# First norm of a layer: TensorE multiplies x by a diagonal of the row factors, in place of scaled copies and transposes

## Chip, cores and metric

One core of one Trainium2 chip. The metric is device time of one execution in microseconds.

## What is computed

A trunk of two layers on 256 tokens of width 1024. Only the first step of each layer is touched by the change:

```python
def rmsnorm(x, g):
    xf = x.astype(jnp.float32)
    y = xf * lax.rsqrt(jnp.mean(xf * xf, axis=-1, keepdims=True) + EPS)
    return (y * g.astype(jnp.float32)).astype(x.dtype)
...
    for l in range(DEPTH):
        h = rmsnorm(x, norm1_g[l])
        x = x + mixing_block(h, ...)      # first product: h @ w_in[l]
        h = rmsnorm(x, norm2_g[l])
        x = x + hier_moe(h, ...)
```

Everything is float32. The matrix products after the norm need h with channels on the partitions, while x is held with tokens on the partitions, so the norm ends in a turn of x by 90 degrees.

## The kernel before

**Tiling.** The tokens are two tiles of 128 (`T = 2`), the channels eight groups of 128 (`KT = 8`). Channel group k is not a run of neighbours: it takes channels k, k + 8, k + 16 and so on, so that a group read straight from x has a step of eight floats (32 bytes) in a partition.

**Split products.** Weights come from memory as float32 "units" of 128 x 2048. ScalarE makes the high part `w_hi` (helper `hi`, line 522), VectorE the low part `w_lo` (helper `lo`, line 839). h is split the same way into `h_hi` and `h_lo` (which live in the tiles `a_hi` and `a_lo`), and each product is three matmuls (lines 1380 to 1382). Each engine's program is written out by hand in its own order, with semaphores between them. No planner is involved: an instruction waits, and all that stands behind it on the same engine waits too.

**The first norm of a layer, step by step.**

1. ScalarE squares x and sums each row (line 545 in layer 0, line 532 in layer 1), after the row tile has been loaded or, in layer 1, after VectorE has added the last sums to x (line 1363).
2. VectorE adds the halves and the epsilon (line 864), GpSimd raises to the power -0.5 (line 464 in layer 0, once per token tile; line 507 in layer 1, both at once). The factor of each row is in `rs1`.
3. The scaled copy `xn` of x is written group by group, x being read with the step of eight: VectorE (line 869) does all of token tile 0 and groups 4 to 7 of tile 1; ScalarE (`scale_part`, line 537) does groups 0 to 3 of tile 1.
4. TensorE transposes the 16 blocks of `xn` (line 1407) into banks 4 to 7 of PSUM: bank 4 + k % 4 holds groups k and k + 4. After the last transposes into a bank the semaphore `n1_t` goes up by one.
5. ScalarE reads the turned groups, multiplies by the gains and writes `h_hi` (line 556). VectorE writes `h_lo` (line 905).
6. TensorE starts the products with `w_in`. In layer 0 the first two units go through `first_products` (lines 1445 to 1456), which first waits for `w_hi` of the unit as a whole and then, for each k, for `h_lo` of that group; eight matmuls with the high weights per k, and those with `w_lo` at the end. In layer 1 it is the ordinary loop (lines 1380 to 1382), twelve matmuls per k.

**Order around it.** While TensorE waits for steps 1 to 3 it multiplies a matrix of ones (`keep_warm`, line 1393): 14 matmuls before the transposes of layer 0, 16 before those of layer 1, and 6 more in layer 0 after the transposes. In layer 0 ScalarE runs `scale_part`, then `hi` of unit 0, then step 5; VectorE does `h_lo` of groups 0 to 3, then `lo` of unit 0, then `h_lo` of groups 4 to 7. In layer 1 the high parts of units 0 and 1 and the low part of unit 0 were made ahead, in the expert part of layer 0. SyncE issues all weight transfers; those of units 0 to 3 come before the norm of layer 0, and the change does not move any.

Of the kernel before, what the change touches and what calls it, by code (L numbers as in the profile page):

```python
# [25 lines left out]
ALU = mybir.AluOpType  # L26
ACT = mybir.ActivationFunctionType
AX = mybir.AxisListType.X

P = 128  # L30
# [10 lines left out]
def trunk(nc, x_in, positions, norm1_g, w_in, sgu_ln_g, sgu_ln_b, sgu_w, sgu_b, q_norm_g, k_norm_g, sinks,  # L41
# [4 lines left out]
    T = SEQ // P  # L46
    KT = D // P
# [65 lines left out]
    with ExitStack() as ctx:  # L113
# [14 lines left out]
        x = sb("x", [P, T, D])  # L128
        a_hi = sb("a_hi", [P, 2048], F32R)
        a_lo = sb("a_lo", [P, 2048], F32R)  # L130
        xn = sb("xn", [P, T, KT, P])
# [33 lines left out]
        ident = sb("ident", [P, P])  # L165
# [19 lines left out]
        rs1 = sb("rs1", [P, T])  # L185
# [43 lines left out]
        diag = flat_g[:, 7168:7168 + SEQ].rearrange("p (t s) -> p t s", t=T)  # L229
# [31 lines left out]
        bank = [ctx.enter_context(nc.psum_tensor(f"bank{i}", [P, 512], F32)) for i in range(8)]  # L261
# [9 lines left out]
        pool_consts = sem("pool_consts")  # L271
# [5 lines left out]
        def S(name):  # L277
            if name not in names:
                names[name] = sem(name)
            return names[name]  # L280
# [233 lines left out]
        def _(act):  # L514
            a = nc.scalar

            def hi(at, n):
                slot = at.raw(n)
                act.wait_ge(landed[slot], at.landed(n))
                act.wait_ge(unit_used, at.ring(n))  # L520
                w = width(n, at.moe)
                a.activation(w_hi[:, at.part(n), 0:w], raw_at(slot)[:, 0:w], ACT.Copy).then_inc(hi_done, 1)  # L522
# [9 lines left out]
                a.activation(sq_dump[:, t, 512 * h:512 * h + 512], x[:, t, 512 * h:512 * h + 512], ACT.Square,  # L532
                             scale=float(D ** -0.5), accum_out=ssqh[:, t, h:h + 1]).then_inc(S("n1_ssq"), 1)

            def scale_part(l):
                act.wait_ge(S("n1_rs"), T * (l + 1))
                a.activation(xn[:, 1, 0:4, :], x[:, 1, :].rearrange("q (p c) -> q c p", c=KT)[:, 0:4, :], ACT.Identity,
                             scale=rs1[:, 1:2]).then_inc(S("n1_xa"), 1)

            act.wait_ge(pool_consts, 1)  # L540
            a.activation(warm[:, 0:1], ones[0:1, 0:1], ACT.Square)
            act.wait_ge(S("ssq_zero"), 1)
            for t in range(T):
                act.wait_ge(x_loaded[t], 16)
                a.activation(sq_dump[:, t, :], x[:, t, :], ACT.Square, scale=float(D ** -0.5),
                             accum_out=ssqh[:, t, 0:1]).then_inc(S("n1_ssq"), 2)
            scale_part(0)
            hi(At(0, 0, False), 0)
            act.wait_ge(S("tab_zero"), 1)
            for l in range(DEPTH):  # L550
                act.wait_ge(par_g, 16 * (l + 1))
                for k in range(KT):
                    act.wait_ge(S("n1_t"), 4 * l + k % 4 + 1)
                    if k >= 4:
                        act.wait_ge(S("h_lo_done"), KT * l + k - 3)
                    a.activation(h_hi[:, k, :], bank[4 + k % 4][:, 256 * (k // 4):256 * (k // 4) + 256], ACT.Identity,
                                 scale=g1[:, k:k + 1]).then_inc(S("h_hi_done"), 1)
                before = act.value_load(tab[0:1, 0, 7:8], min_val=0, max_val=DEPTH * (NG + 1)) if l else 0
                at = At(l, before, False)
                if l == 0:  # L560
# [10 lines left out]
                for t in range(T):  # L571
                    last = a.activation(v_n[:, t, :], bank[1][:, MIX * t:MIX * t + MIX], ACT.Gelu_apprx_tanh,
                                        accum_out=v_mu[:, t:t + 1])
# [80 lines left out]
                for c in range(CT):  # L654
                    a.activation(d_sig[:, c, :], d_acc[:, c, :], ACT.Silu, bias=cols[:, c, K31 + 2:K31 + 3],
                                 scale=cols[:, c, K31 + 1:K31 + 2]).then_inc(S("yd_done"), 1)
# [164 lines left out]
                if l < DEPTH - 1:  # L821
                    for i in range(2 * T):
                        act.wait_ge(S("x_out"), 2 * T * l + i + 1)
                        square(i % 2, i // 2)
                    scale_part(l + 1)

# [2 lines left out]
        def _(dve):  # L831
            v = nc.vector
# [28 lines left out]
            def rstd_rows(l):  # L861
                for t in range(T):
                    dve.wait_ge(S("n1_ssq"), 2 * T * l + (t + 3 if l else 2 * t + 2))
                    v.tensor_scalar(ms1[:, t:t + 1], ssqh[:, t, 0:1], ssqh[:, t, 1:2], EPS, ALU.add,
                                    ALU.add).then_inc(S("n1_ms"), 1)
                for t in range(T):
                    dve.wait_ge(S("n1_rs"), T * l + t + 1)
                    k = 4 * t
                    v.tensor_scalar(xn[:, t, k:, :], x[:, t, :].rearrange("q (p c) -> q c p", c=KT)[:, k:, :],
                                    rs1[:, t:t + 1], None, ALU.mult).then_inc(S("n1_x"), 1)  # L870

            rstd_rows(0)

            def rope_angles():
# [27 lines left out]
            for l in range(DEPTH):  # L902
                for k in range(KT):
                    dve.wait_ge(S("h_hi_done"), KT * l + k + 1)
                    v.scalar_tensor_tensor(out=h_lo[:, k, :], in0=bank[4 + k % 4][:, 256 * (k // 4):256 * (k // 4) + 256],  # L905
                                           scalar=g1[:, k:k + 1], in1=h_hi[:, k, :].bitcast(F32),
                                           op0=ALU.mult, op1=ALU.subtract).then_inc(S("h_lo_done"), 1)
                    if l == 0 and k == 3:
                        lo(At(0, 0, False), 0)

                before = dve.value_load(tab[0:1, 0, 7:8], min_val=0, max_val=DEPTH * (NG + 1)) if l else 0
# [83 lines left out]
                for k in range(K3):  # L995
                    for c in range(CT):
                        w = cols[:, c, K31 + 3 + k:K31 + 4 + k]
                        src = bx[:, c, k:k + SEQ]
                        if k == 0:
                            last = v.tensor_scalar(yc[:, c, :], src, w, None, ALU.mult)  # L1000
                        else:
                            last = v.scalar_tensor_tensor(out=yc[:, c, :], in0=src, scalar=w, in1=yc[:, c, :],
                                                          op0=ALU.mult, op1=ALU.add)
# [352 lines left out]
                for i in range(2 * T):  # L1356
                    t, h = i % 2, i // 2
# [13 lines left out]
        def _(pe):  # L1371
            mm = nc.tensor.matmul
            tp = nc.tensor.transpose
# [17 lines left out]
            def keep_warm(b, n):  # L1391
                for _ in range(n):
                    mm(bank[b][:, 0:P], ones[:, :], ones[:, :], start=True, stop=True)
# [3 lines left out]
            pe.wait_ge(S("zero_done"), 1)  # L1397
            pe.wait_ge(S("tab_zero"), 1)
            for l in range(DEPTH):
                keep_warm(4, 16 if l else 14)  # L1400
                for t in range(T):
                    pe.wait_ge(S("n1_x"), T * l + t + 1)
                    if t:
                        pe.wait_ge(S("n1_xa"), l + 1)
                    for k in (0, 4, 1, 5, 2, 6, 3, 7):
                        c = 256 * (k // 4) + P * t
                        last = tp(bank[4 + k % 4][:, c:c + P], xn[:, t, k, :], ident[:, :])
                        if t == T - 1 and k >= 4:
                            last.then_inc(S("n1_t"), 1)
                if l == 0:  # L1410
                    keep_warm(3, 6)

# [47 lines left out]
                for b in range(4):  # L1460
                    for h in range(2):
# [10 lines left out]
                        for kk in range(4):  # L1472
                            k = 4 * h + kk
                            fi, la = k == 0, k == KT - 1
                            if b == 0:
# [3 lines left out]
                                for t in range(T):  # L1479
                                    last = tokens(1, both(wp, kk, slice(256, 512)), k, t, fi and t == 0, la,  # L1480
                                                  256 * t, 256, True)
                            elif b == 1:
                                for t in range(T):
                                    last = tokens(2 + t, both(wp, kk), k, t, fi, la)
                            else:
                                for f in range(4):
                                    last = channels(2 * (b % 2) + f // 2, wp, k, kk, f, fi, la)
                        last.then_inc(unit_used, 1)
                pe.wait_ge(S("win_act"), 7 * l + 5)
                for h in range(2):  # L1490
                    ready(at, 8 + h)
                    wp = [w[:, 0:4, :] for w in parts(at, 8 + h, "p (c m) -> p c m", c=8)]
                    for kk in range(4):
                        for f in range(2):
                            last = channels(0, wp, 4 * h + kk, kk, f, h == 0 and kk == 0, 4 * h + kk == KT - 1)
# [47 lines left out]
                for h in range(NQ):  # L1543
                    last = score(bank[4][:, P * h:P * h + P], h, 0, 0)
# [4 lines left out]
                for i in range(2):  # L1549
                    for h in (2 * i, 2 * i + 1):  # L1550
                        for tk in range(T):
                            c = 256 * (h % 2) + P * tk
# [139 lines left out]
                for k in range(2):  # L1692
                    last = project_half(1, k)
# [185 lines left out]
```

## Time and profile before

| | us |
|---|---|
| median of 3 runs | 784.68 |
| lowest, highest of the runs | 784.68, 784.87 |
| the profiled execution, its own time | 784.63 |
| its span, first to last instruction | 782.9 |
| granted TensorE clock over the span | 0.999 |
| TensorE busy (matmul) | 772.4 |
| VectorE busy | 646.9 |
| ScalarE busy | 508.1 |

Times in the rows are microseconds from the start of the span, unless marked ns. PE is a matmul on TensorE, PEld the loading of the stationary matrix for it, which overlaps the matmul before; DVE is VectorE, ACT ScalarE, POOL GpSimd, SP SyncE. Ends of matmuls are modelled, so the distance between the starts of neighbours says more than the length of one. The median of the runs and the profiled execution differ by 0.05 us.

### The profile page before, as it was taken

The page shows a single profiled execution, that of the slowest core. Times are in us where ns is not written, and L with a number is a line of the kernel's source. Part 1 is how long each engine was busy: PE and PEld are TensorE (multiplying, and loading weights), DVE is VectorE, ACT ScalarE, POOL GpSimd, SP SyncE. Part 2 cuts the span into 40 slices and gives each one's busy share as a digit, 9 for nine tenths or more (in the row PEclk, how much of TensorE's full clock was granted, in tenths as well). Part 3 has the DMA queues.
Part 4 walks back from the last instruction along what each step waited for, and adds up shares of the span by engine and source line. Part 5 has one row for each costly group of instructions (what it writes and reads, how often), then busy time and mean ns, then how long its engine had stood idle before and what let it go on. Part 6 is the DMA issues. An engine that isn't in the chain of part 4 may idle for free.

```text
span 782.9 us, 13142 instructions
## 1 busy us (share of the span) xinstructions
PE 772.4 (99%) x4850; PEld 690.5 (88%) x4850; DVE 646.9 (83%) x847; ACT 508.1 (65%) x592; POOL 22.6 (3%) x36
## 2 busy tenths in 40 slices
PE   8999999999999999999999999999999999999997
PEld 7899999999878888888889999999988888888885
DVE  5868898469689999897874799757968998989895
ACT  7625646655588778786643655565569877878772
POOL 4020000000000000000001000000000000000000
PEclk9999999999999999999999999999999999999999
DMA  9867254266719999998365624526562999999971
GB/s 303 273 215 241 83 201 137 94 216 216 269 54 328 346 383 335 386 338 276 119 214 204 225 97 173 162 72 239 212 234 90 334 365 386 336 363 352 354 262 54
DMA packets 79499, 186.76 MB, mean 239 GB/s; under 512 B 12470, under 2 KB 24408, under 8 KB 79448
## 3 DMA queue, kind: packets, MB, share of 16 engines
q1 hardware_dynamic: 79448, 186.08, 67.0%
q8 instruction: 32, 0.52, 0.3%
q14 instruction: 19, 0.16, 0.1%
HBM read 185.01 MB, written 1.05 MB: 238 GB/s over the span
## 4 chain that ended last, share of the span: by engine, by line
PE 96%; DVE 1%; ACT 1%; DMA 1%; issue 1%; POOL 0%; DVEq 0%; SPq 0%; ACTq 0%; POOLq 0%
PE bank L1380 28%; PE bank L1382 28%; PE bank L1381 28%; PE bank L1774 2%; PE bank L1685 2%; PE bank L1800 1%; PE bank L1662 1%; PE bank L1539 1%; DMA x<-in_x 1%; PE bank L1445 1%; PE bank L1448 0%; PE bank L1560 0%; PE bank L1564 0%; PE bank L1655 0%; PE bank L1769 0%
## 5 line engine op out<-in xcount | busy, mean ns | idle before, releaser
L839 DVE TENSOR_TENSOR w_lo<-raw,w_hi 128x2048 fp32r<-128x2048 f32 (+1 forms) x144 | 313.5, 2197 | 56.4 <-ACT w_hi L522 55.8
L522 ACT ACTIVATE w_hi<-raw 128x2048 fp32r<-128x2048 f32 (+1 forms) x144 | 264.1, 1844 | 135.3 <-PE bank L1382 131.4
L1380 PE MATMUL bank<-a_hi,w_hi 128*128 128x256 f32 x688 | 195.8, 285 | 0.6 <-DVE a_lo L905 0.6
L1381 PE MATMUL bank<-a_hi,w_lo 128*128 128x256 f32 x688 | 194.6, 283 | 0.0
L1382 PE MATMUL bank<-a_lo,w_hi 128*128 128x256 f32 x688 | 194.6, 283 | 0.0
L1380 PE MATMUL bank<-w_hi,y_lo 128*128 128x512 f32 x432 | 170.9, 395 | 0.0
L1382 PE MATMUL bank<-w_lo,y_lo 128*128 128x512 f32 x432 | 168.6, 390 | 0.0
L1380 PEld LDWEIGHTS bank<-a_hi,w_hi 128*128 128x128 f32 x688 | 131.9, 192 | 1.6 <-issue 1.5
L1381 PEld LDWEIGHTS bank<-a_hi,w_lo 128*128 128x128 f32 x688 | 132.0, 192 | 0.1
L1382 PEld LDWEIGHTS bank<-a_lo,w_hi 128*128 128x128 f32 x688 | 132.0, 192 | 0.0
L1381 PE MATMUL bank<-w_hi,y_hi 128*128 128x512 f32 x288 | 112.3, 390 | 0.0
L1382 PEld LDWEIGHTS bank<-w_lo,y_lo 128*128 128x128 f32 x432 | 81.1, 188 | 17.0
L1380 PEld LDWEIGHTS bank<-w_hi,y_lo 128*128 128x128 f32 x432 | 81.1, 188 | 16.8 <-issue 0.7
L839 DVE TENSOR_TENSOR w_lo<-mid,w_hi 128x2048 fp32r<-128x2048 f32 x36 | 82.2, 2283 | 0.0
L522 ACT ACTIVATE w_hi<-mid 128x2048 fp32r<-128x2048 f32 x36 | 68.8, 1911 | 4.6 <-PE bank L1382 4.6
L1381 PEld LDWEIGHTS bank<-w_hi,y_hi 128*128 128x128 f32 x288 | 54.2, 188 | 10.4
L1381 PE MATMUL bank<-w_hi,y_lo 128*128 128x512 f32 x144 | 56.0, 389 | 0.0
L1020 DVE SCALAR_TENSOR_TENSOR d_acc<-dpad,pcols,d_acc 128x256 f32<-128x256 f32 x120 | 48.5, 479 | 0.0
L1380 PE MATMUL bank<-w_hi,a_hi 128*128 128x512 f32 (+1 forms) x112 | 42.7, 381 | 0.0
L1382 PE MATMUL bank<-w_lo,a_hi 128*128 128x512 f32 (+1 forms) x112 | 41.9, 375 | 0.0
L1381 PE MATMUL bank<-w_hi,a_lo 128*128 128x512 f32 (+1 forms) x112 | 41.9, 374 | 0.0
L766 ACT ACTIVATE y_lo<-bank 128x256 fp32r<-128x256 f32 x36 | 13.8, 384 | 36.3 <-PE bank L1800 36.3
(309 smaller groups left out, 970.4 us busy)
## 6 DMA issues: line engine op xcount, KB each, us to landing
raw<-in_w_e_gate SPq DMA_DIRECT2D x63, 512.0 KB, 4.9
raw<-in_w_e_up SPq DMA_DIRECT2D x63, 512.0 KB, 6.5
raw<-in_w_gate SPq DMA_DIRECT2D x56, 512.0 KB, 4.5
mid<-in_w_e_down SPq DMA_DIRECT2D x54, 512.0 KB, 6.1
raw<-in_w_in SPq DMA_DIRECT2D x32, 512.0 KB, 6.6
raw<-in_w_e_down SPq DMA_DIRECT2D x18, 512.0 KB, 5.0
raw<-in_w_branch SPq DMA_DIRECT2D x16, 512.0 KB, 4.1
raw<-in_w_o SPq DMA_DIRECT2D x16, 512.0 KB, 4.4
```

The source lines that it names most:

```text
L522: a.activation(w_hi[:, at.part(n), 0:w], raw_at(slot)[:, 0:w], ACT.Copy).then_inc(hi_done, 1)
L766: a.activation(hd_hi[:, e % 2, :, :].rearrange("p f s -> p (f s)"), bank[6 + e % 2][:, 0:F], ACT.Copy).then_inc(S("hd_hi_done"), 1)
L839: v.tensor_tensor(w_lo[:, part, 0:w], raw_at(slot)[:, 0:w], w_hi[:, part, 0:w].bitcast(F32), ALU.subtract).then_inc(split_done, 1)
L1020: last = v.scalar_tensor_tensor(out=d_acc[:, c, :], in0=src, scalar=w, in1=d_acc[:, c, :], op0=ALU.mult, op1=ALU.add)
L1380: mm(ps, a2[0], b2[0], start=first, stop=False, skip_group_check=shared)
L1381: mm(ps, a2[1], b2[0], start=False, stop=False, skip_group_check=shared)
L1382: return mm(ps, a2[0], b2[1], start=False, stop=last, skip_group_check=shared)
L1445: mm(bank[0][:, 256 * f:256 * f + 256], wp[0][:, kk, P * f:P * f + P], hp[:, k, :], start=k == 0 and f == 0 and hp is h_hi, stop=False, sk ...
L1539: return mm(ps, qk_t[r, tq, P * (h % 2):P * (h % 2) + P], qk_t[r, tk, 2 * P:3 * P], start=True, stop=True)
L1662: last = mm(bank[small_bank][:, LG[t]:LG[t] + NR], xr[:, t, c, :], wrs[:, c, :], start=c == 0, stop=c == KT - 1, skip_group_check=True)
L1685: return mm(bank[GT_BANKS[k]][:, :], (xt_hi, xt_lo)[i][t][:, k, :], sel[:, t, :], start=t == 0 and i == 0, stop=t == T - 1 and i == 1)
L1774: last = mm(bank[i][:, :], sel_t[:, P * t:P * t + P], zz[:, 512 * h:512 * h + 512], start=False, stop=zz is z_lo, skip_group_check=True)
```

## The change

The scaled copy `xn` is no longer made. VectorE writes, per token tile, a diagonal matrix `diag` with the row factors on it (the identity times `rs1`, 128 x 128). TensorE then takes a block of x as the stationary matrix, read with the step of eight floats, and `diag` as the moving one; the product is the scaled block, turned. It lands where the transpose landed. These are 16 float32 matmuls per layer where there were 16 transposes. `scale_part` is gone from ScalarE.

In layer 0 the eight groups of token tile 0 come first, then those of tile 1 in pairs k, k + 4. In layer 1 TensorE waits for both diagonals, then goes through the pairs with both token tiles. In layer 0 `hi` of unit 0 moves behind `h_hi` of group 2 on ScalarE, and `lo` of unit 0 moves from behind `h_lo` of group 3 to behind `h_lo` of group 2 on VectorE. The matmuls with ones before the turn go from 14 to 11 (layer 0) and from 16 to 14 (layer 1).

```diff
-            def scale_part(l):
-                act.wait_ge(S("n1_rs"), T * (l + 1))
-                a.activation(xn[:, 1, 0:4, :], x[:, 1, :].rearrange("q (p c) -> q c p", c=KT)[:, 0:4, :], ACT.Identity,
-                             scale=rs1[:, 1:2]).then_inc(S("n1_xa"), 1)
...
-            scale_part(0)
-            hi(At(0, 0, False), 0)
             act.wait_ge(S("tab_zero"), 1)
             for l in range(DEPTH):
...
                     a.activation(h_hi[:, k, :], bank[4 + k % 4][:, 256 * (k // 4):256 * (k // 4) + 256], ACT.Identity,
                                  scale=g1[:, k:k + 1]).then_inc(S("h_hi_done"), 1)
+                    if l == 0 and k == 2:
+                        hi(At(0, 0, False), 0)
...
-                    scale_part(l + 1)
...
                 for t in range(T):
                     dve.wait_ge(S("n1_rs"), T * l + t + 1)
-                    k = 4 * t
-                    v.tensor_scalar(xn[:, t, k:, :], x[:, t, :].rearrange("q (p c) -> q c p", c=KT)[:, k:, :],
-                                    rs1[:, t:t + 1], None, ALU.mult).then_inc(S("n1_x"), 1)
-
+                    v.tensor_scalar(diag[:, t, :], ident[:, :], rs1[:, t:t + 1], None, ALU.mult).then_inc(S("n1_x"), 1)
+
+            dve.wait_ge(pool_consts, 3)
             rstd_rows(0)
...
-                    if l == 0 and k == 3:
+                    if l == 0 and k == 2:
                         lo(At(0, 0, False), 0)
...
-                keep_warm(4, 16 if l else 14)
-                for t in range(T):
-                    pe.wait_ge(S("n1_x"), T * l + t + 1)
-                    if t:
-                        pe.wait_ge(S("n1_xa"), l + 1)
-                    for k in (0, 4, 1, 5, 2, 6, 3, 7):
-                        c = 256 * (k // 4) + P * t
-                        last = tp(bank[4 + k % 4][:, c:c + P], xn[:, t, k, :], ident[:, :])
-                        if t == T - 1 and k >= 4:
-                            last.then_inc(S("n1_t"), 1)
+                keep_warm(4, 14 if l else 11)
+
+                def scaled_turn(t, k):
+                    c = 256 * (k // 4) + P * t
+                    return mm(bank[4 + k % 4][:, c:c + P], x[:, t, :].rearrange("q (p c) -> q c p", c=KT)[:, k, :],
+                              diag[:, t, :], start=True, stop=True, skip_group_check=True)
+
+                if l == 0:
+                    pe.wait_ge(S("n1_x"), 1)
+                    for k in range(KT):
+                        scaled_turn(0, k)
+                    pe.wait_ge(S("n1_x"), T)
+                    for k in range(4):
+                        scaled_turn(1, k)
+                        scaled_turn(1, k + 4).then_inc(S("n1_t"), 1)
+                else:
+                    pe.wait_ge(S("n1_x"), T * (l + 1))
+                    for k in range(4):
+                        for kk in (k, k + 4):
+                            for t in range(T):
+                                last = scaled_turn(t, kk)
+                        last.then_inc(S("n1_t"), 1)
```

## Rows read from the trace of the kernel before

**Rows 1.** The page of the profile: span, TensorE, chain that ended last.
```profile
span 782.9 us, 13142 instructions
...
PE 772.4 (99%) x4850; PEld 690.5 (88%) x4850; DVE 646.9 (83%) x847; ACT 508.1 (65%) x592; POOL 22.6 (3%) x36
...
PE 96%; DVE 1%; ACT 1%; DMA 1%; issue 1%; POOL 0%; DVEq 0%; SPq 0%; ACTq 0%; POOLq 0%
```

**Rows 2.** Stretches: length, then busy us (count) of PE, PEld, DVE, ACT, POOL, granted clock, DMA.
```profile
13.00:207.00 194.00, 193.94 (x1518) 186.86 (x1518) 155.44 (x233) 106.26 (x135) 8.86 (x6) 1.00 0.58 193
...
382.00:580.00 198.00, 197.94 (x1539) 190.25 (x1538) 153.34 (x211) 107.30 (x137) 3.53 (x3) 1.00 0.54 183
```

**Rows 3.** Timeline of the weight loads, start of the kernel; start, length, engine.
```profile
2.05 4.77 PEld L1393 LDWEIGHTS bank<-ones 128*128 128x128 f32 x22 [2.05 <-POOL mhalf L454]
...
6.91 0.70 PEld L1393 LDWEIGHTS bank<-ones 128*128 128x128 f32 x5
```

**Rows 4.** Timeline of layer 0, all engines; start us, length us, engine.
```profile
7.14 1.14 DVE L869 TENSOR_SCALAR xn<-x,rs 128x1024 f32<-128x1024 f32 x1
7.31 1.39 POOL L464 TENSOR_TENSOR rs<-ms,mhalf 128x1 f32<-128x1 f32 x1 [0.75 <-DVE ms L864]
...
8.33 1.09 PE L1407 MATMUL bank<-ident,xn 128*128 128x128 f32 x8 [0.53 <-DVE xn L869]
...
9.86 1.90 ACT L522 ACTIVATE w_hi<-raw 128x2048 fp32r<-128x2048 f32 x1
...
10.10 1.06 PE L1407 MATMUL bank<-ident,xn 128*128 128x128 f32 x8 [0.68 <-ACT xn L537]
...
11.00 1.50 PE L1393 MATMUL bank<-ones 128*128 128x128 f32 x12
...
11.66 3.02 ACT L556 ACTIVATE a_hi<-bank,g 128x256 fp32r<-128x256 f32 x8
...
12.15 1.66 DVE L905 SCALAR_TENSOR_TENSOR a_lo<-bank,g,a_hi 128x256 fp32r<-128x256 f32 x4 [2.72 <-ACT a_hi L556]
...
12.78 0.48 PE L1445 MATMUL bank<-a_hi,w_hi 128*128 128x256 f32 x2 [0.28 <-DVE a_lo L905]
...
13.73 2.28 DVE L839 TENSOR_TENSOR w_lo<-raw,w_hi 128x2048 fp32r<-128x2048 f32 x1
...
14.54 0.40 PE L1448 MATMUL bank<-w_hi,a_lo 128*128 128x256 f32 x2
```

**Rows 5.** Timeline of the boundary to layer 1, all engines.
```profile
374.46 3.73 PE L1393 MATMUL bank<-ones 128*128 128x128 f32 x32
...
377.12 0.70 POOL L507 TENSOR_TENSOR rs<-ms,mhalf 128x2 f32<-128x2 f32 x1 [156.53 <-DVE ms L864]
...
377.85 1.75 DVE L869 TENSOR_SCALAR xn<-x,rs 128x1024 f32<-128x1024 f32 x2 [0.88 <-POOL rs L507]
...
379.05 1.97 PE L1407 MATMUL bank<-ident,xn 128*128 128x128 f32 x16 [0.86 <-DVE xn L869]
380.46 3.03 ACT L556 ACTIVATE a_hi<-bank,g 128x256 fp32r<-128x256 f32 x8 [1.39 <-PE bank L1407]
...
381.60 0.36 PE L1380 MATMUL bank<-a_hi,w_hi 128*128 128x256 f32 x1 [0.58 <-DVE a_lo L905]
```

**Rows 6.** VectorE groups by shape: busy us, mean ns of one.
```profile
L869 DVE TENSOR_SCALAR xn<-x,rs 128x1024 f32<-128x1024 f32 x2 | 2.3, 1140 | 0.9 <-POOL rs L507 0.9
...
L1174 DVE TENSOR_SCALAR y_hi<-iota,d_acc 128x512 fp32r<-128x512 f32 x4 | 1.9, 487 | 0.1
...
L937 DVE TENSOR_SCALAR mid<-mid,v_mu 128x256 f32<-128x256 f32 x4 | 1.4, 355 | 0.1
L869 DVE TENSOR_SCALAR xn<-x,rs 128x512 f32<-128x512 f32 x2 | 1.4, 698 | 0.5 <-POOL rs L464 0.5
```

**Rows 7.** ScalarE groups by shape.
```profile
L532 ACT ACTIVATE gates<-x 128x512 f32<-128x512 f32 x4 | 2.5, 622 | 1.4 <-DVE x L1363 1.4
L537 ACT ACTIVATE xn<-x,rs 128x512 f32<-128x512 f32 x2 | 2.5, 1225 | 2.9 <-POOL rs L464 1.8 <-POOL rs L507 1.1
```

## The prediction

> **What bounds the kernel now.** I read the page first: TensorE is busy for 772.4 of 782.9 us, and 96% of the chain that ended last is its own [rows 1]. The stretches behind the two norms say it more sharply: 193.94 of 194 us and 197.94 of 198 us [rows 2]. So a delay of TensorE's first product in a layer is handed on to the end one for one, and work taken from VectorE or ScalarE gains nothing unless TensorE was waiting for it. The timelines show where it did. In layer 0 the first product starts at 12.78 [rows 4]. What holds it is ScalarE: the split of unit 0 runs from 9.86 to 11.76, only then comes `h_hi` at 11.66 (the records overlap a little), `h_lo` at 12.15, and the product. The transposes' second batch began at 10.10 and was no longer the last. In layer 1 the chain is another: GpSimd ends at 377.82, VectorE copies from 377.85, transposes from 379.05, `h_hi` at 380.46, first product at 381.60 [rows 5]. The change touches these two stretches, 7 to 13 us and 378 to 382 us, and nothing else.
>
> **Price of a turn.** Transposes are one record each: 8 took 1.06 us, the last being 0.27 long, so they follow at 0.113 us. A float32 matmul of the same size is two records: the 16 matmuls with ones of layer 1 are 32 records in 3.73 us, the last 0.27 long, so 0.112 us apart [rows 5]. So 16 turns cost 32 x 0.112 = 3.58 us where 16 transposes cost 1.8. The Trainium skill says as much in Perfetto Trace Analysis, Transposes: use the transpose and not a standard matmul, since it skips the arithmetic; the trace agrees, with 1 record against 2, and the sum is made from the records.
>
> **Price of a diagonal.** No row has it. VectorE's `tensor_scalar` took 487 ns for 512 columns and 355 ns for 256 [rows 6], 0.52 ns a column, so 0.29 us for 128. It replaces copies of 1.14 and 0.70 us.
>
> **Layer 0.** VectorE starts the first diagonal where it started the copy, 7.14, and ends at 7.43; TensorE followed the copy by 0.05 us, so it starts at 7.48 instead of 8.33. The second diagonal waits for GpSimd, which even at its old 1.39 us [rows 4] ends at 8.70, so that the diagonal is there by 9.05, before the 16 records of tile 0 are through at 9.27. That wait costs nothing. ScalarE may turn to unit 0 only after `h_hi` of group 2, and this needs the third pair of tile 1, the 28th record: it starts at 7.48 + 27 x 0.112 = 10.50. From a matmul's start to the reader's was 0.39 us (tenth transpose at 379.05 + 9 x 0.113, `h_hi` at 380.46 [rows 5]), so `h_hi` of group 2 starts at 10.89. ScalarE's eight follow at 0.36 us (3.02 us less a last one of 0.49, over 7), so the split of unit 0 starts at 11.25, where it started at 9.86, and ends 1.90 later at 13.15. `first_products` waits for it: TensorE starts at 13.20. That is **0.42 us later** than 12.78. What was hidden behind it stays so: `lo` of unit 0 goes ahead of `h_lo` of group 3 and holds VectorE for 2.28 us [rows 4], so `h_lo` 3 (0.4 us more, by four in 1.66) ends at about 15.9; TensorE wants it after 24 matmuls. The pair at 14.54 is the eighth from 12.78, so a matmul takes 0.125 us, and that is at 16.2. If that slack of 0.3 us goes, the price is what it is short by. `w_lo` of unit 0 is wanted only after 32 matmuls, 17.2. The six matmuls with ones behind the turns end by 12.6, in the wait. ScalarE's unit 1 slips from 14.52 to about 16.3 and ends at 18.2, wanted at 13.20 + 48 x 0.125 = 19.2.
>
> **Layer 1.** GpSimd's start is not touched. Two diagonals from 377.85 take 0.58 us less an overlap of 0.09 (1.14 + 0.70 against 1.75 in the row), to 378.34; TensorE starts at 378.39 instead of 379.05. Its 32 records end at 381.97. `h_hi` 0 is free after eight records and `h_lo` 0 is done near 380.3, so the first product waits for nothing but TensorE itself and starts at 381.97: **0.37 us later** than 381.60. The chain by way of ScalarE and VectorE is no longer the last, the turns are. `h_lo` 1 is wanted 12 matmuls of 0.125 us on, at 383.5, and is ready. The fillers, 14 for 16, end at 377.8 and wait for nothing.
>
> **Copies removed.** VectorE loses 1.84 us per layer and gains 0.5, ScalarE loses 1.23 [rows 7]. Both are off the path behind the norm, by rows 2's near-full TensorE, so this is worth nothing. No transfer moves; SyncE's and GpSimd's orders stay. Removing ScalarE's 1.23 us in layer 0 only lets it wait earlier for the turns.
>
> **Sum.** 784.63 + 0.42 + 0.37 = 785.4 us for the profiled execution, and the median of the runs, 784.68, lies 0.05 from it: no difference.
>
> **The unknown: reading x with a step as the stationary matrix.** No load in the trace has a step. From below it costs nothing (0.112 us a record; it can't gain, since a contiguous load sets that pace already). From VectorE's rows: with the step, 512 more columns took 442 ns, 0.86 ns each [rows 6], 0.110 us for 128, which is no price at all; its whole row, 1140 ns for 1024 columns, makes 0.143 us for 128. From ScalarE's rows: 1225 ns with the step against 622 ns without, for 512 columns [rows 7], 1.18 ns more each, 0.151 us more per record. I take nothing, because a load at 0.112 us asks for a column every 0.87 ns, which is what VectorE got. The Trainium skill speaks against it in Advanced Engine Details and Errata, SBUF Cachelines: full speed needs two hits on a line of 16 bytes, another line at each access is penalized; a step of 32 bytes never hits twice. It names no figure; the sum by it is that of the first rival below. ScalarE's row agrees with it, and VectorE's does in part.
>
> **Rivals.**
> - *Slow loads*, the case on the other side. Each of the 32 loads takes ScalarE's surcharge. Layer 0: 27 x 0.151 = 4.1 us more; layer 1: 32 x 0.151 = 4.8 more; with 0.8 from above 794.3 us. Above 0.125 us a record it decides: 59 records of 0.013 us more and the 0.8 from above pass 0.2%. For it: ScalarE doubled. Against it: VectorE at the very pace a load needs. 0.12. Its mild form, 0.143 us a record, adds 27 x 0.031 + 32 x 0.031 = 1.8: 787.2. 0.07.
> - *Late clock.* In layer 0 the loads follow at 0.21 us up to 6.9 and at half that behind [rows 3], which I read as the step from 1.2 to 2.4 GHz. The fillers now end near 7.05 and TensorE stands until 7.48, close to where it rose. If it stays at 1.2 GHz through the turns, 27 x 0.10 = 2.7 us more, 788.1; if it rises midway, 786.8. Against it: the work before 6.9 is the same. 0.07.
> - *Cheap turns.* If the second record of a turn cost nothing, the turns would be as short as the transposes and start earlier: layer 0 by 14 x 0.112 less, 11.64 (-1.1), layer 1 at `h_lo` 0, 380.24 (-1.4): 782.1. Against it: the fillers are the same instruction and show both records at full distance. I leave it 0.08, also for a gain that no row shows me.
>
> **How the numbers follow.** My forecast has 0.66, its own range 784.9 to 785.9 (a diagonal at 0.2 or 0.4 us, or the slack of 0.3 gone). The whole range, 784.2 to 788.1, takes in the late clock and the mild form of the slow loads, and leaves out the full one and the cheap turns, 0.20. A measurement of this kernel can tell 0.2% from no change, 1.6 us. Slower: 0.12, the late clock's 0.07, and most of the mild form, 0.05: 0.24. Faster: 0.08. Same: 0.68.
>
> **What would show it.** The two stretches behind the norms as long as before. Turns at 0.112 us between records, 32 per layer: at 0.26 the slow loads are right, at 0.21 in layer 0 alone the late clock. First product of layer 0 just behind ScalarE's unit 0, near 13.2; that of layer 1 directly behind the last turn, near 382.0. A TensorE wait at group 3 of layer 0 would mean that the slack was less than nothing. The prediction is wrong if TensorE waits in the 190 us behind a norm where it did not before, or if layer 1's turns end before `h_lo` 0.

## The result, and the profile after

| | before | changed |
|---|---|---|
| median, us | 784.77 (4 runs) | 793.84 (4 runs) |
| lowest, highest | 784.68, 787.08 | 793.02, 794.63 |
| profiled execution, its span | 784.63, 782.9 | 794.63, 792.9 |

The ratio is 1.0108, with a 95% interval of 1.0093 to 1.0122: 1.1% slower. The forecast was 785.4, the range 784.2 to 788.1. The measured time lies outside it, 0.5 us from the 794.3 us of the rival that was called slow loads. One execution of e5, the profiled one, and one of the kernel before took twice their usual time (1537 us); they are left out, and no row of e5's profile is read.

The page of the changed kernel: span, busy time, and the chain that ended last, by engine and by line.

```profile
span 792.9 us, 13183 instructions
...
PE 784.2 (99%) x4872; PEld 702.6 (89%) x4872; DVE 644.9 (81%) x847; ACT 506.0 (64%) x590; POOL 19.4 (2%) x36
...
PE 96%; DVE 1%; ACT 1%; DMA 0%; issue 0%; POOL 0%; DVEq 0%; ACTq 0%; POOLq 0%
PE bank L1373 28%; PE bank L1375 28%; PE bank L1374 28%; PE bank L1397 2%; PE bank L1779 2%; PE bank L1690 2%; PE bank L1805 1%; PE bank L1667 1%; PE bank L1544 1%; PE bank L1450 1%; PE bank L1453 0%; DMA x<-in_x 0%; PE bank L1565 0%; PE bank L1569 0%; PE bank L1660 0%; ACT gates L532 0%
```

TensorE is busy 784.2 us against 772.4 [rows 1], and a line that is not in the old chain is now fourth in it: L1397, the turns, with 2% of the span.

The timeline of layer 0 (start us, length us, engine), the rows that answer to [rows 4]:

```profile
7.20 0.28 DVE L862 TENSOR_SCALAR gates<-ident,rs 128x128 f32<-128x128 f32 x1
...
7.36 0.55 POOL L464 TENSOR_TENSOR rs<-ms,mhalf 128x1 f32<-128x1 f32 x1 [0.46 <-DVE ms L858]
...
7.53 7.89 PE L1397 MATMUL bank<-gates,x 128*128 128x128 f32 x32 [0.41 <-DVE gates L862]
...
7.95 0.30 DVE L862 TENSOR_SCALAR gates<-ident,rs 128x128 f32<-128x128 f32 x1 [0.47 <-POOL rs L464]
...
14.50 0.47 ACT L549 ACTIVATE a_hi<-bank,g 128x256 fp32r<-128x256 f32 x1 [0.48 <-PE bank L1397]
14.87 1.90 ACT L522 ACTIVATE w_hi<-raw 128x2048 fp32r<-128x2048 f32 x1
...
15.25 1.50 PE L1386 MATMUL bank<-ones 128*128 128x128 f32 x12
...
16.83 0.50 PE L1450 MATMUL bank<-a_hi,w_hi 128*128 128x256 f32 x2
```

VectorE's part came as forecast: a diagonal takes 0.28 us (estimate 0.29), the turns start at 7.53 (7.48). Then 32 records take 7.89 us, the last 0.40 long: 0.242 us apart where the forecast had 0.112. `h_hi` of group 2 comes at 14.50 instead of 10.89, unit 0's split at 14.87, and the first product at 16.83. It was at 12.78 before: **4.05 us later**.

The boundary to layer 1, the rows that answer to [rows 5]:

```profile
378.52 3.29 PE L1386 MATMUL bank<-ones 128*128 128x128 f32 x28
...
381.18 0.70 POOL L507 TENSOR_TENSOR rs<-ms,mhalf 128x2 f32<-128x2 f32 x1 [156.50 <-DVE ms L858]
381.91 0.48 DVE L862 TENSOR_SCALAR gates<-ident,rs 128x128 f32<-128x128 f32 x2 [0.88 <-POOL rs L507]
...
382.45 7.89 PE L1397 MATMUL bank<-gates,x 128*128 128x128 f32 x32 [0.64 <-DVE gates L862]
384.72 0.47 ACT L549 ACTIVATE a_hi<-bank,g 128x256 fp32r<-128x256 f32 x1 [3.93 <-PE bank L1397]
...
390.09 0.36 PE L1373 MATMUL bank<-a_hi,w_hi 128*128 128x256 f32 x1
```

GpSimd starts 4.06 us later than before (381.18 against 377.12), which is layer 0's loss handed on one for one. The first product comes 8.91 us behind it, where it was 4.48: **4.43 us more**. It follows the last turn at once. Together 8.5 us, while the spans differ by 10.0. The other 1.5 us are behind layer 1's norm. The stretches there (length, busy us and count of PE, PEld, DVE, ACT, POOL, granted clock, DMA share, GB/s):

```profile
468.00:472.00 4.00, 4.00 (x33) 2.71 (x31) 3.79 (x7) 2.88 (x6) 0.00 (x0) 0.99 0.02 4
472.00:476.00 4.00, 4.00 (x23) 4.00 (x22) 3.97 (x4) 3.61 (x17) 0.00 (x0) 0.58 0.10 13
476.00:480.00 4.00, 4.00 (x36) 4.00 (x35) 4.00 (x9) 0.90 (x3) 0.00 (x0) 1.00 0.99 365
```

From 472 to 476 TensorE gets through 23 matmuls instead of 36, and the granted clock is 0.58 on average: it stood at the lower of its two levels, 1.2 GHz, for most of these 4 us. At 36 in 4 us, the 13 missing are 1.4 us. The profiled execution of before has no such fall there. Such a fall is not the change's doing. The runs of the changed kernel with a mean clock of 0.999 are at 793.02 and 793.10, those with 0.998 at 794.57 and 794.63, and the kernel before splits in the same way, as the last part shows. So the change costs 8.4 us, comparing runs without a fall (793.0 to 793.1 against 784.7), and 8.5 us by the two timelines.

### The profile page after: what moved, and what is told of

It is laid out like the page before. It is cut to its first block, busy times and chain, and to the rows that moved or that the text cites. A ratio compares the mean times of both kernels' runs of the same rounds, so it can differ in the third digit from the quotient of the medians.

```text
span 792.9 us, 13183 instructions
## 1 busy us (share of the span) xinstructions
PE 784.2 (99%) x4872; PEld 702.6 (89%) x4872; DVE 644.9 (81%) x847; ACT 506.0 (64%) x590; POOL 19.4 (2%) x36
## 4 chain that ended last, share of the span: by engine, by line
PE 96%; DVE 1%; ACT 1%; DMA 0%; issue 0%; POOL 0%; DVEq 0%; ACTq 0%; POOLq 0%
PE bank L1373 28%; PE bank L1375 28%; PE bank L1374 28%; PE bank L1397 2%; PE bank L1779 2%; PE bank L1690 2%; PE bank L1805 1%; PE bank L1667 1%; PE bank L1544 1%; PE bank L1450 1%; PE bank L1453 0%; DMA x<-in_x 0%; PE bank L1565 0%; PE bank L1569 0%; PE bank L1660 0%; ACT gates L532 0%
```

## The experiments

Theory A: the stationary read of x with a step of 32 bytes makes each load 0.13 us longer. Theory B: something else in these products does (the diagonal, the banks, float32 data other than ones). Eight kernels were run.

**e1: the turns without the step.** A channel group becomes 128 neighbours, and the weights that meet h (`w_in`, `w_gate`) and the gains are loaded in the matching row order; of each statement only its first line is shown:

```diff
-    return mm(bank[4 + k % 4][:, c:c + P], x[:, t, :].rearrange("q (p c) -> q c p", c=KT)[:, k, :],
+    return mm(bank[4 + k % 4][:, c:c + P], x[:, t, P * k:P * k + P],
-    s = w_in[l].rearrange("(p c) m -> p c m", c=KT)[...]
+    s = w_in[l].rearrange("(c p) m -> p c m", p=P)[...]
...
```

> The changed kernel, but a channel group is 128 neighbours instead of every eighth channel: the turns read x without a step, and w_in, w_gate and the gains are loaded in the matching row order (pieces of 2 KB as before; the gains in pieces of 4 bytes). Theory A, the step of the stationary read makes each of the 64 loads 0.13 us longer: the turns' records follow at 0.112 us, first products at 13.2 and about 382.4, time about 785.4. Theory B, the float32 product with a diagonal is slow whatever the step (its operands, its banks): records stay at 0.24 us and the time at 793 to 794.6.

Measured: 785.58 and 785.66 in the two runs with clock 1.000, 786.81 in the median of ten (the others have a clock of 0.997 or 0.998). Against before the ratio is 1.0013 (0.9995 to 1.0031). The timeline, layer 0 and then the boundary:

```profile
7.52 3.84 PE L1398 MATMUL bank<-gates,x 128*128 128x128 f32 x32 [1.38 <-DVE gates L863]
...
11.32 1.90 ACT L523 ACTIVATE w_hi<-raw 128x2048 fp32r<-128x2048 f32 x1
...
13.28 0.50 PE L1451 MATMUL bank<-a_hi,w_hi 128*128 128x256 f32 x2 [0.58 <-ACT w_hi L523]
```

```profile
377.68 0.70 POOL L508 TENSOR_TENSOR rs<-ms,mhalf 128x2 f32<-128x2 f32 x1 [156.55 <-DVE ms L859]
...
378.95 3.84 PE L1398 MATMUL bank<-gates,x 128*128 128x128 f32 x32 [0.65 <-DVE gates L863]
...
382.55 0.36 PE L1374 MATMUL bank<-a_hi,w_hi 128*128 128x256 f32 x1
```

32 records in 3.84 us, the last 0.27 long: 0.115 us apart. The diagonal, the banks, the float32 data and the matmul count are those of the changed kernel, only the step is gone, and with it 0.127 of the 0.130 us. Theory B falls. The first product of layer 0 is at 13.28 (forecast 13.20), that of layer 1 comes 4.87 us behind GpSimd's start, 0.39 more than before (forecast 0.37). So with the step gone the rest of the prediction's sum holds: 785.4 us was forecast, 785.58 and 785.66 were measured.

**e2: the old copies without the step.** The same row order in the kernel before; `x[:, t, :]` is copied as it lies.

> The kernel before (scaled copies and transposes) with the same row order, so that the copies read x without a step. Theory A (a step costs on more engines than one): ScalarE's copy falls from 1.23 to 0.62 us, VectorE's from 1.14 to about 0.75 and from 0.70 to 0.49; layer 0 gains 0.6 us (ScalarE turns to unit 0 sooner), layer 1 0.4: about 783.7. Theory B: the copies stay as long as they were, 784.7.

Measured: 783.36 and 783.72 at a clock of 0.999 or more, median 785.13 of ten (eight with 0.998 or less), ratio 0.9994 (0.9984 to 1.0004). Its timeline in layer 0:

```profile
7.26 0.74 DVE L870 TENSOR_SCALAR xn<-x,rs 128x1024 f32<-128x1024 f32 x1
7.42 0.99 POOL L465 TENSOR_TENSOR rs<-ms,mhalf 128x1 f32<-128x1 f32 x1 [0.62 <-DVE ms L865]
...
8.45 0.73 ACT L538 ACTIVATE xn<-x,rs 128x512 f32<-128x512 f32 x1 [1.35 <-POOL rs L465]
...
9.08 1.90 ACT L523 ACTIVATE w_hi<-raw 128x2048 fp32r<-128x2048 f32 x1
...
12.00 0.48 PE L1446 MATMUL bank<-a_hi,w_hi 128*128 128x256 f32 x2 [0.28 <-DVE a_lo L906]
```

VectorE's copy takes 0.74 us instead of 1.14, ScalarE's 0.73 instead of 1.23 [rows 4, 7], and the first product comes at 12.00 instead of 12.78. So the step had cost VectorE too: 0.40 us for 1024 columns. ScalarE's copy did not fall to the 0.62 us that was expected, which was the length of its squares, another operation; the first product still gained 0.78 us where 0.6 was expected, because ScalarE's copy also starts 0.28 us sooner (8.45 for 8.73). It waits for GpSimd, whose power of tile 1 is done at 8.41 instead of 8.70: both times about 0.41 us behind the end of VectorE's copy. At the boundary the first product comes 0.39 us sooner behind GpSimd's start (expected 0.4). The time at equal clock is about 1.2 us lower than that of the kernel before, but only two of the ten runs have that clock, and the interval reaches over 1.

**e3: eight steps side by side.** The changed kernel with these products behind the turns of layer 0, once for each step s of 1 to 8:

```diff
+    for _ in range(8):
+        mm(bank[3][:, 0:P], x[:, 0, 0:128 * s].rearrange("q (p c) -> q c p", c=s)[:, 0, :], ones[:, :], start=True, stop=True)
```

> The changed kernel with 64 float32 matmuls more in layer 0 behind the turns: x as the stationary matrix, ones as the moving one, eight matmuls (16 records) at each step of 1 to 8 floats. They write a bank that is cleared before use. Theory A: 0.112 us between records at step 1 and 0.24 at step 8; if what counts is a line of 16 bytes, up to step 2 (two floats in a line) nothing is lost, and from 4 on each load costs the same. Theory B: 0.112 us at every step. The time grows by 7.2 us (B) to about 13 us (A).

Measured, in one run: 819.13 us, 24.5 more than the changed kernel's profiled execution. The expectation counted 64 records, and 64 float32 matmuls are 128, so the times in it were half of what they should have been. The loads, one row per step in rising order; the start of the next row less the start of this one, over 16, is the distance:

```profile
16.43 1.87 PEld L1419 LDWEIGHTS bank<-ones,x 128*128 128x128 f32 x16
18.22 1.97 PEld L1421 LDWEIGHTS bank<-ones,x 128*128 128x128 f32 x16
20.10 2.85 PEld L1423 LDWEIGHTS bank<-ones,x 128*128 128x128 f32 x16
22.87 3.82 PEld L1425 LDWEIGHTS bank<-ones,x 128*128 128x128 f32 x16
26.59 3.67 PEld L1427 LDWEIGHTS bank<-ones,x 128*128 128x128 f32 x16
30.16 3.68 PEld L1429 LDWEIGHTS bank<-ones,x 128*128 128x128 f32 x16
33.75 3.83 PEld L1431 LDWEIGHTS bank<-ones,x 128*128 128x128 f32 x16
37.48 3.90 PEld L1433 LDWEIGHTS bank<-ones,x 128*128 128x128 f32 x16
41.28 0.32 PEld L1467 LDWEIGHTS bank<-a_hi,w_hi 128*128 128x128 f32 x2
```

| step in floats | 1 | 2 | 3 | 4 | 5 | 6 | 7 | 8 |
|---|---|---|---|---|---|---|---|---|
| us per record | 0.112 | 0.118 | 0.173 | 0.233 | 0.223 | 0.224 | 0.233 | 0.238 |

Two floats apart is nearly free, three cost half of the surcharge, four cost all there is to pay, and from there on the distance doesn't matter. The sum of the table, times 16, is 24.9 us, close to the 24.5 by which the kernel grew. The Trainium skill (Advanced Engine Details and Errata, SBUF Cachelines) says that two hits are needed on a line of 16 bytes for full speed. This table agrees with it: at step 2 a line still holds two of the floats read, at step 4 one. Step 3 fits as well: its reads fall on three lines for every four floats, and 0.75 x 0.233 us is 0.175 (an estimate from the table), where 0.173 was measured.

**e4: the moving side, and transposes.** In the same place, ones stationary and x moving at steps 1, 2, 4, 8, then transposes of x at the same steps (16 each).

> The changed kernel with 32 matmuls and 64 transposes more in layer 0 behind the turns: ones stationary and x moving at steps of 1, 2, 4 and 8 floats (eight matmuls each), then transposes of x at steps of 1, 2, 4 and 8 (sixteen each). Theory A, if any read of TensorE suffers from the step: moving records go from 0.112 to 0.24 us or so, and transposes likewise, so that a transpose of x with a step of 8 costs 0.24 us. If only stationary reads of a matmul suffer, the moving ones stay at 0.112. Theory B: all at 0.112.

Measured, in one run: 814.25 us, 19.6 more than the changed kernel's profiled execution. The matmul records of TensorE, four rows of moving reads and four of transposes:

```profile
16.68 1.95 PE L1419 MATMUL bank<-x,ones 128*128 128x128 f32 x16
18.47 1.98 PE L1421 MATMUL bank<-x,ones 128*128 128x128 f32 x16
20.29 3.79 PE L1423 MATMUL bank<-x,ones 128*128 128x128 f32 x16
23.90 3.91 PE L1425 MATMUL bank<-x,ones 128*128 128x128 f32 x16
27.63 1.93 PE L1427 MATMUL bank<-ident,x 128*128 128x128 f32 x16
29.40 2.08 PE L1429 MATMUL bank<-ident,x 128*128 128x128 f32 x16
31.31 2.09 PE L1431 MATMUL bank<-ident,x 128*128 128x128 f32 x16
33.23 1.98 PE L1433 MATMUL bank<-ident,x 128*128 128x128 f32 x16
34.97 0.48 PE L1467 MATMUL bank<-a_hi,w_hi 128*128 128x256 f32 x2
```

| step in floats | 1 | 2 | 4 | 8 |
|---|---|---|---|---|
| x moving, us per record | 0.112 | 0.114 | 0.226 | 0.233 |
| transposes of x, us per record | 0.111 | 0.119 | 0.120 | 0.109 |

The moving read pays like the stationary one. A float32 transpose pays next to nothing: at step 8 it takes 0.109 us, and it is one record. Why it is spared no run shows.

The same profile has the turns of layer 0 partly at the lower clock. First the turns in the timeline, then two stretches (the columns as in the stretches of the result):

```profile
7.60 7.90 PE L1397 MATMUL bank<-gates,x 128*128 128x128 f32 x32 [0.52 <-DVE gates L862]
```

```profile
7.60:10.30 2.70, 2.70 (x11) 2.70 (x12) 0.30 (x1) 0.00 (x0) 2.21 (x7) 1.00 1.04 389
10.30:13.60 3.30, 3.30 (x15) 3.30 (x15) 0.24 (x1) 0.48 (x1) 2.28 (x12) 0.51 1.06 394
```

The granted clock was 0.51 in the second stretch, in the middle of the turns, and yet the 32 records took 7.90 us, against 7.89 in the changed kernel's profile with the clock at 1.00. By this one stretch TensorE's clock does not set the pace of the read with a step. No record without a step lies in it that could confirm the clock, and the granted clock of a profile is not exact everywhere: it reads 1.00 in the first 6 us of the changed kernel too, where the loads of ones are still 0.21 us apart.

**e5: copies in x's own order, the step moved into the transpose.** No weight is loaded otherwise.

```diff
-    a.activation(xn[:, 1, 0:4, :], x[:, 1, :].rearrange("q (p c) -> q c p", c=KT)[:, 0:4, :], ACT.Identity,
+    a.activation(xnf[:, D:D + D // 2], x[:, 1, 0:D // 2], ACT.Identity,
...
-    v.tensor_scalar(xn[:, t, k:, :], x[:, t, :].rearrange("q (p c) -> q c p", c=KT)[:, k:, :],
+    v.tensor_scalar(xnf[:, D * t + P * k:D * t + D], x[:, t, P * k:],
...
-    last = tp(bank[4 + k % 4][:, c:c + P], xn[:, t, k, :], ident[:, :])
+    last = tp(bank[4 + k % 4][:, c:c + P], xnf[:, D * t:D * t + D].rearrange("q (p c) -> q c p", c=KT)[:, k, :],
+              ident[:, :])
```

> The kernel before, but the scaled copies are written in x's own order (read and written without a step), and the transposes read them with the step of eight floats. No weight is loaded otherwise. Theory A in its narrow form (a step costs in a float32 matmul's stationary or moving read and in ScalarE's and VectorE's copies, not in a transpose): transposes stay at 0.11 to 0.12 us a record, copies fall to 0.74 and 0.73 us, first products 0.5 to 0.8 us earlier in layer 0 and about 0.3 in layer 1: 783.6 in runs whose clock is 1.000, against 784.4 to 785.1 of the kernel before. Rival: a transpose's step costs like a matmul's, 0.24 us a record, 16 records: 2 us slower per layer, 787.

Measured: of eight runs with a clock of 0.999 or 1.000 seven lie at 783.42 to 783.73 and one at 784.35; the median of all is 783.70. The kernel before, on the same chip, had 784.23 to 784.80 at that clock in 15 of 16 runs, and a median of 784.80. That is about 1.1 us less, as expected, but the interval of the ratio, 0.9991 (0.9976 to 1.0006), reaches over 1. How long its transposes take is read from e6, which has the same ones.

**e6: and unit 0's split first.** VectorE copies both tiles whole in layer 0, ScalarE splits unit 0 right behind the squares, 2 matmuls with ones follow the transposes instead of 6. The edit against e5:

```diff
-            scale_part(0)
             hi(At(0, 0, False), 0)
...
-                    k = 4 * t
+                    k = 4 * t if l else 0
...
-                    if t:
-                        pe.wait_ge(S("n1_xa"), l + 1)
+                    if t and l:
+                        pe.wait_ge(S("n1_xa"), l)
...
-                    keep_warm(3, 6)
+                    keep_warm(3, 2)
```

> As e5, and in layer 0 VectorE copies both token tiles whole, ScalarE splits unit 0 right behind the squares (before it, the scaled copy), and 2 matmuls with ones instead of 6 follow the transposes. If the chain of layer 0 was held by unit 0's split on ScalarE, that split now starts when its transfer has landed, near 8.4, and the first product comes at 11.0 to 11.4 instead of 12.0: 783.0 at clock 1.000. Rival: the transfer lands later than 9, or the clock falls in the gap behind the fewer fillers: 783.6 or more.

Measured: 783.36 in the median of twelve, ratio 0.9985 (0.9976 to 0.9993): faster than both kernels, by 0.15% of the kernel before. Its timeline in layer 0 and at the boundary:

```profile
8.73 1.91 ACT L522 ACTIVATE w_hi<-raw 128x2048 fp32r<-128x2048 f32 x1 [1.63 <-DMA raw<-in_w_in]
...
10.55 3.01 ACT L555 ACTIVATE a_hi<-bank,g 128x256 fp32r<-128x256 f32 x8
...
11.67 0.48 PE L1445 MATMUL bank<-a_hi,w_hi 128*128 128x256 f32 x2 [0.79 <-DVE a_lo L904]
```

```profile
375.95 0.70 POOL L507 TENSOR_TENSOR rs<-ms,mhalf 128x2 f32<-128x2 f32 x1 [156.50 <-DVE ms L863]
...
377.50 2.05 PE L1406 MATMUL bank<-ident,xn 128*128 128x128 f32 x16 [0.46 <-DVE xn L868]
...
380.11 0.36 PE L1379 MATMUL bank<-a_hi,w_hi 128*128 128x256 f32 x1 [0.57 <-DVE a_lo L904]
```

The split starts when the transfer has landed, 8.73, the gains follow it at 10.55, and the first product is at 11.67, 1.11 us sooner than before. It was hoped for at 11.0 to 11.4; the transfer lands 0.3 us later than I had put it. The clock did not fall behind the two fillers. At the boundary 16 transposes at step 8 take 2.05 us, the last 0.28 long: 0.118 us apart, where those without a step were 0.113. The first product comes 4.16 us behind GpSimd's start, 0.32 sooner than before. The two gains make 1.43 us, and the runs at a clock of 0.999 or 1.000 agree: 783.04 to 783.80, middle 783.25, against 784.68 of the kernel before.

**e7: e1 with unit 0's split where it was.**

> e1 (turns by the diagonal, x read without a step), with unit 0's split put back where the kernel before has it: on ScalarE ahead of the gains, on VectorE behind group 3. If the first product of layer 0 waits for that split, as the prediction said, it now waits for the turns and the six fillers behind them instead, and starts near 12.5 where e1 has 13.28: 0.8 us less, 784.8 at clock 1.000. Rival: the order is worth nothing, 785.6.

Measured: 784.62, 784.70, 784.84 and 785.34 at a clock of 0.999 or 1.000, against 785.58 and 785.66 of e1; median 786.10 of ten, with six runs at 0.998 or less. The two ran on different chips, on which the kernel before had 784.7 us in the middle at that clock alike. In the profiled executions the first product of layer 0 comes at 12.63 where e1 has 13.28, although the turns start later (7.69 against 7.52, x having come later). So the moved split was what the first product waited for in the changed order, as the prediction said, and it cost 0.65 us, or 0.82 counted from the first turn. What comes last in its place are the turns and the six fillers behind them.

**e8: fillers among the small products.**

> The kernel before with 8 matmuls with ones (16 records, 1.8 us per layer) more, between the attention scores and the spatial gating products, in a bank that is free there. In the runs so far whose mean clock is 0.998 or less, TensorE stood at half its clock for about 3.4 us, each time just behind these small products. If the low activity of that stretch is the cause, all runs now have clock 1.000 and lie at 784.7 + 3.6 = 788.3, within 0.7 us of each other. If the falls are chance or come from elsewhere, half of the runs stay at 0.998 and 1.5 us more.

Measured: 788.72 and 788.73 at clock 1.000, 789.45 and 790.13 at 0.998. The 16 records per layer cost 4.0 us where 3.6 were expected, and two of four runs still have a fall. In the profiled one it is no longer behind the scores but in the router's stretch, among matmuls of 4 to 20 columns, transposes and gathers (the columns as in the stretches of the result):

```profile
592.00:596.00 4.00, 4.00 (x19) 3.31 (x19) 2.08 (x9) 4.00 (x3) 1.05 (x1) 0.71 0.32 130
```

This does not decide it: the fall left the place that was filled and came up in another, but four runs are few. Nor did every fall before e8 lie behind the small products, as its expectation says: e4's in the turns of layer 0 did not.

## Why the prediction was wrong

**What bounds the kernel** was right. Layer 0's loss of 4.05 us was found whole at the boundary (4.06), and nothing between absorbed it. No new wait of TensorE appeared behind the norms: it is busy for 193.94 of the 194 us from 17.00 and for 197.85 of the 197.91 from 390.09.

**The parts other than the load** were right to a tenth: the diagonal 0.28 us for 0.29; start of the turns 7.53 for 7.48; with the step removed (e1) the first products at 13.28 for 13.20 and 0.39 for 0.37 us more. That the removed copies are worth nothing in this order is borne out: VectorE and ScalarE do less in e1 than before, and e1 is no faster. The chain that replaced the copies is TensorE's own, two records a turn, as the price of a turn had it. The mechanism by which the reordering costs (ScalarE's split of unit 0 becomes last) is shown by e7. One size was wrong and cost nothing: the power of tile 1 on GpSimd was left at 1.39 us and took 0.55.

**The step that failed is "I take nothing"**, the price of the stationary read with a step. It stood between 0.112 us a record and 0.263 (0.151 more), and was 0.242, close to the upper end. 27 x 0.130 = 3.5 us with the 0.4 from the sum makes 3.9 for layer 0 (measured 4.05); 32 x 0.130 = 4.2 with 0.4 makes 4.5 for layer 1 (measured 4.43). Together 8.5, and the sum of 785.4 less 0.8 plus that is 793.1, the time of the runs without a fall.

How the reading went astray can be said exactly. I compared VectorE's pace with the step, 0.86 ns a column, with what a load needs, 0.87, and called it "no price at all". The right comparison was with VectorE's own pace without the step, and that stood in the same group: 0.52 ns a column [rows 6]. VectorE had slowed by a factor of 1.65 a column, ScalarE from 622 to 1225 ns [rows 7], e2 shows that both were the step's doing. The page of the Trainium skill that the prediction names spoke for the surcharge as well. Two groups of rows and that page were for it, one misread row was against it, and 0.12 was too little for it.

The rows could not have given its size, though. TensorE's surcharge, 0.130 us over 128 columns, is 1.02 ns a column. Like for like, copy against copy in e2, the step cost ScalarE 0.98 ns a column (0.50 us for 512) and VectorE 0.39 (0.40 us for 1024). ScalarE's is close and VectorE's is not, and why, no run shows; the 1.18 ns of the prediction, which set ScalarE's copy against its squares, was near by luck.

**The rivals.** Slow loads was right, with its size off by 0.021 us a record. Over 59 records that is 1.2 us, the distance of its 794.3 from the runs without a fall; that the median of all runs lies only 0.5 from it is chance, since two of the four had a fall that adds 1.5. Late clock did not cost anything: the 32 turns of layer 0 take 7.89 us like those of layer 1. By e4 that alone does not tell the clock, but in e1, without the step, both take 3.84, so there it had risen by the first turn. Cheap turns did not either: 32 records per layer.

## What to carry to other kernels

Before a matmul reads float32 with a step of four or more (16 bytes), either operand, price the record double, as measured here for 128 columns from step 4 on. Whether a step costs anything is to be judged by what it cost another engine against that engine's own plain rows, not by its absolute pace; how much it costs has to be measured on the engine itself (here 0.39, 0.98 and 1.02 ns a column on three engines). If data must be turned out of such an order, let the transpose take the step (0.109 us at step 8) and keep the copy ahead of it plain (0.74 for 1.14 us); e5 did this alone, and its gain is not clear of its interval; e6, which also moves the split of unit 0 up, was 0.15% faster. Where TensorE is busy to the last, work moved to it from engines with slack has to be paid in full: here 16 transposes became 32 records even before the step.

## What the runs showed of the hardware that was not expected

- The step costs a float32 matmul but next to nothing for a float32 transpose (e4, e6), on the same data in the same tile.
- The read with a step did not slow down with TensorE's clock in the one stretch where both met (e4, granted clock 0.51, 0.24 us a record as at 1.00), while at the start of the kernel loads without a step went at 0.21 us and then at 0.112.
- GpSimd's power of one column took 1.39 us beside VectorE's copy of 1.14, 0.99 beside one of 0.74 (e2), and 0.55 beside the diagonal of 0.28. Each time it ended 0.41 to 0.43 us behind VectorE's operation, so a longer copy on VectorE went with a later start of ScalarE's copy, which waits for GpSimd (8.73 before, 8.45 in e2). Why, no run shows.
- TensorE's clock falls to the lower level for some microseconds, once or several times, in a good part of the executions, also of the kernel before. Of 28 runs of it beside e5 to e8, 16 have a mean clock of 0.999 or 1.000 and lie at 784.23 to 785.41 us, 12 have 0.998 or less and lie at 785.75 to 787.34; beside e1 to e4, on another chip, 10 of 19 have 0.998 or less. Of the falls that the profiles show, six lie just behind the attention scores and the gating products (changed kernel at 472, e2 at 94, e3 at 496, e4 at 116 and 491, e7 at 94), where TensorE's weight loads had been busy for 2.7 to 2.9 of the 4 us ahead of the fall; in the profile of the kernel before the same stretches passed without a fall at 2.9 of 4 us (90 to 94, 458 to 462). Two lie elsewhere (e4 at 10.3, e8 at 594). e8 did not settle whether filling the stretch helps. Medians of a few runs can differ by 1.5 us for this alone, which is more than e5's gain; runs of equal mean clock are the ones to compare.
